# Early first projections and products across the array's halves in two recurrent stages of a fused transformer kernel

## What is computed

```python
z_na, z_gla, z_rw = hn @ w[:, :2048], hn @ w[:, 2048:3616], hn @ w[:, 3616:]
# gated linear attention, two directions, 4 heads (dk 64, dv 128), chunks of 64 tokens
b = cumsum(log_sigmoid(gd @ g_up + g_b) / 16)          # gd: the low-rank columns of z_gla
qe, ke, kd = q * exp(b), k * exp(-b), k * exp(b_last - b)
o = tril(qe @ ke.T) @ v + qe @ S_prev;  S = exp(b_last) * S_prev + kd.T @ v
# delta rule (rwkv7), two directions, 8 heads of 64
zs = conv3(z_rw)                                        # over tokens, three taps
r, k, v, wd, ad = split(zs); decay = f(tanh(wd) @ w_up); alpha = sigmoid(ad @ a_up)
S = S * w_t + (S @ a_t) b_t + v_t k_t;  y = S @ r_t
```

## Time and profile before

| | us |
|---|---|
| Three runs: median | 4121.07 |
| lowest, highest | 4120.27, 4122.79 |
| The profiled execution, its own time | 4117.64 |
| its span, first to last instruction | 4115.8 |
| PE busy in it | 3879.8 (94%) |
| DVE, ACT, POOL busy | 1526.1, 1061.7, 376.6 |
| Mean granted clock of PE | 0.977 |

### The profile page before, as it was taken

How to read it: one execution, slowest core, us unless ns; L and a number is a source line. 1 busy time by engine, 2 the same in 40 slices (tenths; PEclk the granted TensorE clock), 3 DMA queues, 4 the chain that set the end, 5 groups by cost and what they waited for, 6 DMA issues and landing times. The chain is left out here.

```text
span 4115.8 us, 64473 instructions
## 1 busy us (share of the span) xinstructions
PE 3879.8 (94%) x27772; PEld 2141.4 (52%) x27772; DVE 1526.1 (37%) x3218; ACT 1061.7 (26%) x2295; POOL 376.6 (9%) x533
## 2 busy tenths in 40 slices
PE   8999999898989889999989999999999989999998
PEld 4556755666675744544554444444444444444443
DVE  2233334464646512135658111113356547111113
ACT  2333113333343401125541000003253321000003
POOL 3340002011101000000100000000001000000000
PEclk9999999999999999999999999999999999999999
DMA  4101101000000031211048899997211148899997
GB/s 106 32 21 39 32 27 42 13 18 13 22 9 22 4 124 57 50 37 25 1 154 314 290 329 316 314 323 257 95 44 31 51 164 316 297 326 309 324 319 247
DMA packets 320587, 567.28 MB, mean 138 GB/s; under 512 B 53504, under 2 KB 127392, under 8 KB 320304
## 3 DMA queue, kind: packets, MB, share of 16 engines
q1 hardware_dynamic: 304832, 506.01, 36.3%
q0 software_dynamic: 9504, 34.61, 3.5%
q10 hardware_dynamic: 5968, 22.55, 1.4%
HBM read 514.85 MB, written 48.23 MB: 137 GB/s over the span
## 5 line engine op out<-in xcount | busy, mean ns | idle before, releaser
L3536 PE MATMUL bank<-ring,m_picked_T 128*128 128x512 f32 x2048 | 897.2, 596 | 4.1 <-ACT m_picked_T L3619 4.1
L3536 PEld LDWEIGHTS bank<-ring,m_picked_T 128*128 128x128 f32 x2048 | 389.0, 191 | 481.4 <-issue 475.8
L3536 PE MATMUL bank<-ring,m_hidden_T 128*128 128x512 f32 x1024 | 455.3, 593 | 0.0
L3536 PEld LDWEIGHTS bank<-ring,m_hidden_T 128*128 128x128 f32 x1024 | 189.6, 190 | 215.5 <-issue 215.5
L3785 DVE TENSOR_TENSOR m_hidden<-m_hidden,bank 128x512 f32<-128x512 f32 x64 | 44.0, 687 | 506.7 <-ACT m_hidden L3625 506.7
L1561 PE MATMUL bank<-hnT,first_block 128*128 128x336 f32 (+3 forms) x544 | 180.5, 483 | 8.0 <-PEq L101 7.3
L3625 ACT ACTIVATE m_hidden<-bank 128x512 f32<-128x512 f32 x64 | 38.2, 597 | 538.9 <-PE bank L3536 538.9
L241 PE MATMUL bank<-xT,first_block 128*128 128x512 f32 x352 | 152.4, 593 | 2.6 <-ACT l_i L3264 1.7
L3915 POOL DMA_INDIRECT y_rows<-m_ys,m_tokens x30 | 47.7, 1589 | 1111.9 <-DVE m_ys L3800 1046.4
L2820 PE MATMUL bank<-xT,a_weights 128*128 128x512 f32 x320 | 142.3, 595 | 0.8 <-ACT xT L2676 0.8
L1561 PEld LDWEIGHTS bank<-hnT,first_block 128*128 128x128 f32 x544 | 102.1, 193 | 67.6 <-issue 20.9
(11 more groups left out here) (503 smaller groups left out, 6010.0 us busy)
## 6 DMA issues: line engine op xcount, KB each, us to landing
ring<-in_moe_w_gate_up SPq DMA_DIRECT2D x512, 512.0 KB, 7.5
ring<-in_moe_w_down SPq DMA_DIRECT2D x256, 512.0 KB, 4.6
first_block<-in_w_in SPq DMA_DIRECT2D x23, 512.0 KB, 3.8
w_block<-in_w_in SPq DMA_DIRECT2D x19, 512.0 KB, 3.8
x_rows<-X ACTq DMA_DIRECT2D x2, 4096.0 KB, 17.0
ring<-y_rows SPq DMA_DIRECT2D x16, 512.0 KB, 8.3
out_w<-in_w_out ACTq DMA_DIRECT2D x11, 512.0 KB, 12.5
first_block<-in_lru_w_in SPq DMA_DIRECT2D x11, 512.0 KB, 3.9
```

The source lines that it names most:

```text
L3536: m = pe.matmul(banks[j][:, :], lhsT[:, (i % 8) * P:(i % 8 + 1) * P], ring[:, i, j, :], start=i % 8 == 0, stop=i % 8 == KD - 1)
```

## The change

Three things are done.

First, the three low-rank products of GLA are issued in attention's last three turns, into banks 4, 5 and 0; GLA begins with the value products, and ACT copies the finished low-rank spans. SP's waits change with the counts.

Second, five of the six spans of the delta rule's first two blocks are issued in GLA's tail: one before the first sums, one between the sums, three behind them. The sixth is the delta rule's first product. ACT copies all six in the new stage, from banks 7, 3, 4, 5, 6, 2. Key products into banks 0 and 1 wait no longer for a raw copy; into bank 2 for all six.

Third, products across the halves stand beside diagonal ones. In GLA the transposes of the keys are written in the other half, and ACT copies them back for direction 0 by two half copies, for direction 1 straight; the values get a second copy with swapped halves (`swapped`), by two more half copies each; direction 0's outer products are diagonal, direction 1's go across with the swapped values. Scores and transposes alternate, and so do the outer products. In the chain of the delta rule the output products go across and alternate with the state's, and the chained y addition becomes two operations of 64 partitions per direction.

```diff
+LOW_BANKS = (4, 5, 0)
+RAW_BANKS = ((7, 3, 4), (5, 6, 2))
...
+        def low_rank_tensor(pe, t):
+
+            j = t - steps
+            (col, w), to = SPANS[j], LOW_BANKS[j]
+            if j == 0:
+                pe.wait_ge(*k.first_in[0].now())
+            pe.wait_ge(o_taken.sem, (2 * (steps - 2), 2 * (steps - 2), 2 * (steps - 1))[j])
+            for d in range(KD):
+                x = pe.matmul(ps[to][0:48, 0:w], low_rank(k)[:, d, :], hnT[:, d, col:col + w], start=d == 0, stop=d == KD - 1)
+            x.then_inc(*k.early.up())
...
                     scores_tensor(pe, t)
+                else:
+                    low_rank_tensor(pe, t)
...
+        def raw_tensor(pe, i, j):
+
+            col, n = SPANS[j]
+            for d in range(KD):
+                x = pe.matmul(ps[RAW_BANKS[i][j]][:, 0:n], k.first[i][:, d, :], hnT[:, d, col:col + n], start=d == 0,
+                              stop=d == KD - 1)
+            x.then_inc(*k.early.up())
...
+            if j:
                 pe.wait_ge(turn_copied.sem, 5 * p + j)
...
             for i, ch in enumerate(chunks_of(j)):
                 for d in range(2):
-                    for h in HALF:
-                        x = pe.matmul(t[h, d, i, :], ke[d][h, tokens(ch)], c["ident"][h, h])
-            x.then_inc(*turned.up())
+                    for h in range(2):
+                        if j:
+                            x = pe.matmul(b[HALF[h], d, i, :], ke[d][HALF[h], tokens(ch)], qe[d][HALF[h], tokens(ch)])
+                        y = pe.matmul(t[HALF[1 - h], d, i, :], ke[d][HALF[h], tokens(ch)], c["ident"][HALF[h], HALF[h]])
...
-            for d in range(2):
-                for i, ch in enumerate(chunks_of(j)):
-                    for h in HALF:
-                        x = pe.matmul(ps[5 + d][h, i * P:i * P + P], kT[(5 * p + j) % 2][h, d, i, :], V[p][h, ch, :])
-                x.then_inc(*outer.up())
+            for i, ch in enumerate(chunks_of(j)):
+                for h in range(2):
+                    x = pe.matmul(ps[5][HALF[h], i * P:i * P + P], kT[(5 * p + j) % 2][HALF[h], 0, i, :], V[p][HALF[h], ch, :])
+                    y = pe.matmul(ps[6][HALF[h], i * P:i * P + P], kT[(5 * p + j) % 2][HALF[1 - h], 1, i, :],
+                                  swapped[p][HALF[1 - h], ch, :])
...
         def tensor(pe):
-            gd_tensor(pe)
             v_tensor(pe, 0, 0)
...
-            sum_tensor(pe, 1)
+            pe.wait_ge(*k.first_in[0].now())
+            raw_tensor(pe, 0, 0)
+            sum_tensor(pe, 1, [0])
+            pe.wait_ge(o_copied.sem, 6)
+            pe.wait_ge(squared.sem, 6)
+            raw_tensor(pe, 0, 1)
+            sum_tensor(pe, 1, [1])
+            raw_tensor(pe, 0, 2)
+            pe.wait_ge(o_copied.sem, 8)
+            pe.wait_ge(squared.sem, 8)
+            pe.wait_ge(*k.first_in[1].now())
+            raw_tensor(pe, 1, 0)
+            raw_tensor(pe, 1, 1)
...
+            ac.activation(V[p][:, chunks, :], b, ACT.Copy)
+            ac.activation(swapped[p][HALF[0], chunks, :], b[HALF[1]], ACT.Copy)
+            ac.activation(swapped[p][HALF[1], chunks, :], b[HALF[0]], ACT.Copy).then_inc(*done("v", p, j, 0))
...
+            for h in range(2):
+                ac.activation(kT[(5 * p + j) % 2][HALF[h], 0, 0:n, :], t[HALF[1 - h], 0], ACT.Copy)
+            ac.activation(kT[(5 * p + j) % 2][:, 1, 0:n, :], t[:, 1], ACT.Copy).then_inc(*turn_copied.up())
...
             cols = [RW0 + 3 * BW, RW0 + 3 * BW + P]
-            ends = [3, 6]
+            ends = [0, 1]
...
-                pe.wait_ge(copied.sem, 1 + j)
+                pe.wait_ge(copied.sem, 6 if j == 2 else 1)
...
                     pe.matmul(s_bank[HALF[h], d, :], L.P1[HALF[h], d, at[d], :], S[HALF[h], d, :])
-            for d in range(2):
-                for h in range(2):
-                    x = pe.matmul(y_bank[HALF[h], d, at[d], :], S[HALF[h], d, :], L.Q[HALF[h], d, at[d], :])
+                    x = pe.matmul(y_bank[HALF[1 - h], d, at[d], :], S[HALF[h], d, :], L.Q[HALF[h], d, at[d], :])
...
-            for i in range(2):
-                block_tensor(pe, i, ps[3 * i:3 * i + 3], enumerate(SPANS))
+            block_tensor(pe, 1, [ps[x] for x in RAW_BANKS[1]], [(2, SPANS[2])])
...
+                if chained:
+                    ve.tensor_tensor(part[HALF[0]], bank[HALF[1]], part[HALF[0]], ALU.add)
+                    ve.tensor_tensor(part[HALF[1]], bank[HALF[0]], part[HALF[1]], ALU.add).then_inc(*y_added.up())
```

More of the change, by code:

```diff
@@ L783, in gla_branch @@
         wb = [k.first[1]] + [st.sb(f"w_block{i}", [P, KD, P]) for i in range(1, 3)]
-        wv, w_low, ahead = st.sb("w_values", [P, KD, 2 * P]), low_rank(k), k.first_in[0].now()
+        wv = st.sb("w_values", [P, KD, 2 * P])
         gd, up = st.sb("gla_gd", [48, COLS]), st.sb("gla_up", [48, 2 * P])
@@ L817, in bank @@
         def bank(*name):
-            return ps[number[name] % 3]
+            return ps[(number[name] + 1) % 3]
         def reads(name):
@@ L865, in load_block, with next_block @@
             sp.dma_start(wb[i % 3][:, :, :], w3[:, :, blocks[i][2]:blocks[i][2] + P]).then_inc(*w_in[i % 3].up(16))
-        def next_block(sp, i, unit):
-            sp.wait_ge(made.sem, unit + 1)
+        def next_block(sp, i):
+            if i:
+                sp.wait_ge(made.sem, last_unit(max(b for b in range(len(blocks)) if b % 3 == 0)) + 1)
             col = RW0 + 3 * BW + i * P
@@ L893, in sync @@
             load_values(sp, 1)
-            next_block(sp, 0, number["gd", 0, 2, 0])
+            next_block(sp, 0)
             for i in range(3, len(blocks)):
                 load_block(sp, i)
-            next_block(sp, 1, last_unit(max(i for i in range(len(blocks)) if i % 3 == 0)))
+            next_block(sp, 1)
             for p in range(PAIRS):
@@ L1019, in read_tensor, with sum_tensor @@
             x.then_inc(*read.up())
-        def sum_tensor(pe, p):
-            for j in range(2):
+        def sum_tensor(pe, p, spans=range(2)):
+            for j in spans:
                 for h in range(2):
@@ L1081, in v_scalar @@
             n = len(chunks_of(j))
[L1082 to L1083 removed]
+            chunks, b = slice(chunks_of(j)[0], chunks_of(j)[-1] + 1), bank("v", p, j, 0)[:, 0:n * P].rearrange("p (c v) -> p c v", v=P)
+            ac.activation(V[p][:, chunks, :], b, ACT.Copy)
+            ac.activation(swapped[p][HALF[0], chunks, :], b[HALF[1]], ACT.Copy)
+            ac.activation(swapped[p][HALF[1], chunks, :], b[HALF[0]], ACT.Copy).then_inc(*done("v", p, j, 0))
         def log_scalar(ac, p, d):
@@ L1136, in scalar @@
             for j, (col, n) in enumerate(SPANS):
-                ready(ac, "gd", 0, j, 0)
-                ac.activation(gd[:, col:col + n], bank("gd", 0, j, 0)[0:48, 0:n], ACT.Copy).then_inc(*done("gd", 0, j, 0))
+                ac.wait_ge(k.early.sem, j + 1)
+                ac.activation(gd[:, col:col + n], ps[LOW_BANKS[j]][0:48, 0:n], ACT.Copy).then_inc(*gd_copied.up())
             for j in range(2):
@@ L1437, in spans_done @@
         def spans_done(p, block):
-            return 6 + 11 * p + (3, 6, 9, 11)[block]
+            return 1 + 11 * p + (3, 6, 9, 11)[block]
         def copies_done(p, block):
@@ L2188, in scalar @@
             ac.wait_ge(padded.sem, 8)
-            for j in range(2):
-                copy_raw(ac, temps(0)[1 + j], ps[3 * j:3 * j + 3], 3 * j, copied)
+            for i in range(2):
+                for j, (col, n) in enumerate(SPANS):
+                    if (i, j) == (1, 2):
+                        ac.wait_ge(projected.sem, 1)
+                    else:
+                        ac.wait_ge(k.early.sem, 3 + 3 * i + j + 1)
+                    ac.activation(temps(0)[1 + i][:, 1 + col:1 + col + n], ps[RAW_BANKS[i][j]][:, 0:n], ACT.Copy).then_inc(*copied.up())
             ac.wait_ge(mixed_in.sem, 3)
```

47 lines of the change are left out of this document (17 added, 30 removed).

## The result

The changed kernel takes 4099.4 us (median of four, 4098.6 to 4101.8) against 4121.9 (4120.3 to 4123.4): ratio 0.9948, 95% interval 0.9932 to 0.9964, that is 22.5 us less, with 15 to 28 inside the interval. I had put 34 less, 4087, with a range of 4075 to 4102. The sign and the range hold, a third of the gain is missing. At the first product behind the delta rule (1470.01 before, 1451.99 after) the two traces are 18.0 apart; the rest of the program, which the change does not touch, ran 2.3 us longer in the changed trace.

What follows compares the result with a forecast made beforehand. TensorE (PE), busy 94% of the span, was taken as the bound. Terms -2.7 -8.7 -14.8 -7.8 = -34.0 took the profiled 4117.64 us to 4083.6; with 3.4 for the median, 4087, range 4075 to 4102.

Steps and rivals of the forecast that it cites:

- Products across the halves: GLA's score, transpose and outer products: four quarters in a round double the pace, -14.8 us.
- Rival 1: GLA and chain: neighbours sharing a row group wait for each other, so nothing doubles; 4113 us, chance 0.09.
- rival 4: Quarter products in the new order run one at a time, making the kernel slower: 4170 us, chance 0.03.
- Second border: GLA to delta rule: five spans issued early remove PE's pause of 7.3 us; -8.7 us in all.
- rival 3: Second border: the stage's preamble or key weights come late, five of the 8.7 us lost; 4092 us, chance 0.03.
- First border: Attention to GLA: three low-rank products move ahead of the border, V products then end earlier; -2.7 us in all.
- +0.5: First border: two added half copies of V delay the second low product about 1.2 us; net cost 0.5 us.
- rival 2: GLA: ACT's added copies make it the bound, up to 15 us lost; 4102 us, chance 0.07.
- The chain: Delta rule's chain: 64 steps go from 8 rounds to 4, 14.9 us saved, not all arriving; -7.8 us.
- 3.7 x 3/4 + 3.5: Chain: 3.7 us saved by main-loop steps followed by PE's own work, 3.5 between pairs after y additions.
- (c): Chain's last eight steps: savings partly doubled by half clock, less the costs of y additions; 0.6 us gained.
- 0.7 for the last y and 0.3 for an earlier y: Chain's end: cost in us of divided y additions, the earlier one standing ahead of the inverse's addition.

Runs made afterwards that it cites:

- gla_only: Kernel before, with products across the halves and their copies in the gated linear attention alone: 4106.2 us, ratio 0.9965.
- the two repairs: Changed kernel, with either the key block's first two spans not waiting for the first raw copy (4090.8 us) or POOL's padding written before its masks (4090.2 us).
- burst: Kernel before, plus 2688 extra quarter products in eight orders and widths behind GLA's last sums, results unused: four quarters at 64 columns 16 ns busy a record.
- y_split: Kernel before, chain left on the diagonal, each chained y addition divided into two on half the partitions: 4123.3 us, ratio 1.0010.
- chain_only: Kernel before, with only the delta rule's chain changed, four quarters in a round and divided y additions: 4116.3 us, ratio 0.9986.
- chain_back: Changed kernel, with the delta rule's chain on the diagonal again in all pairs and y additions undivided: 4102.8 us, ratio 0.9953.
- both: Changed kernel, key block's first two spans waiting for no raw copy and V bank free after the first copy: 4089.3 us, ratio 0.9927.
- all_diag: Kernel `both`, with all four pairs' chains on the diagonal and no divided y addition: 4098.6 us, ratio 0.9939.
- k_free: Changed kernel, the key block's first two spans no longer waiting for ACT's first raw copy: 4090.8 us, ratio 0.9925.
- the dense run above: Last run inside `burst`, 1024 products on four quarters at 64 columns: 56.10 us for 2053 records, 27 ns a record.

## Why the prediction was right and where it was wrong

**Products across the halves: right.** Forecast -14.8. From the first group of score products to the last sums the trace shows 626.71 - 456.93 before and 611.18 - 456.16 after (where the first early projection now stands), 14.76 less, and the same in every kernel that has these products; each round holds four, a group of scores and transposes saves 0.93 and an outer group 0.87, and `gla_only` measured 14.4. Rival 1 and rival 4 fall with it, and so does the row-group rule of the Trainium skill, "TensorE: Matmul & The Clock Gate", Part 3 (The mechanism), for this order: sharing rows or not gave the same 16 ns.

**Second border: the pause went, the gain did not.** Forecast -8.7, measured -1.3 (from the last sums' start to the low-rank products 55.47 before, 54.17 after), and -8.3 with either of the two repairs. The step that failed is "ACT's first raw copy waits for POOL's padding until 8.6 us after the stage's start ... then end at 671.2, two microseconds before they are wanted". It asked when the convolutions are wanted and not who else waits for the copies: the diff had `copied.sem, 6 if j == 2 else 1` for the key block, in plain sight. That is rival 3, which I gave 0.03 and five of 8.7 us; it took 7.4. Barrier, last span, weights and key block were right to 0.1: with the wait gone it is 19.06 us, forecast 19.0.

**First border: short by 3.5.** Forecast -2.7; from record 1900, in the attention's tail, to the second low product of pair 1 the changed kernel takes 0.8 us more than before. The pause was right; the stage begins 1.4 late against my sum. The term "+0.5" for the V copies was mis-sized: alone they cost 1.0 (`gla_only` 99.9 against 98.9; but `burst`, without them, has 99.4), and beside the early products 2 to 3. With the bank freed early the border gives -1.7 to -2.6, close to my sum. This is the small, local form of rival 2. Its large form falls: no other wait on those copies shows.

**The chain: two parts right, the last wrong.** In the first three pairs I had 3.7 x 3/4 + 3.5 = 6.3 and measured 6.9. For the last pair, loop and (c), I had -1.5 and measured +2.3. The terms "0.7 for the last y and 0.3 for an earlier y" are 1.14 and 1.27 (2.4 against 1.2, 2.2 against 0.9): the last pair has no other pair's projections behind which DVE's additions could hide. And there is more time at half clock in that pair, 18 us on average against 11; the divided additions alone do not bring it (`y_split` has 10), and what sets it off was not tried. In sum -4.6 by the means, forecast -7.8. The whole times say much the same of the whole chain: 5.8 (`chain_only`), 2 (the changed kernel against `chain_back`) and 5 (`both` against `all_diag`) by the ratios, the first with some 4 us of doubt, the others with 8.

The parts as measured, +0.8 -1.3 -14.8 -4.6, make -19.9, within the interval of the measured -22.5. Two mis-sized terms and one overlooked wait make up the difference to -34. The two traces themselves also hold 1.6 us between the first border and the first scores (before, 3.4 us at half clock; after, none), which is scatter, as `k_free` shows. That the range held is in part luck: its high end was made for a chain that saves nothing or for ACT's 15 us, and what used it up was above all a wait that I had given 0.03. The measured 4099.4 lies 2.6 below that end.

## What to carry to other kernels

When work is moved ahead of a stage's border, follow each of the next stage's waits back to its releaser: whatever used to be ready before it was wanted (here POOL's padding, queued behind its masks) may now be late, and a wait that once cost nothing may guard nothing. Order a stage's setup by who wants it first. A trick that divides another engine's work, as the additions to y, belongs only where that engine has cover: here, by the means, it pays in three pairs and costs in the fourth.

## What the runs showed that was not expected

PE's instructions reach it in blocks: that is how three things read together, a stall at every 128th product record, no releaser for it, and the queue below. In the dense run above, 128 product records and their weight loads take 3.45 to 3.75 us to arrive, 27 ns a record, just under the pace of two quarters (29) and well over that of four (15 to 16). The queue for instructions on the page, before and with the burst (packets, MB, share):
```profile
q8 instruction: 220, 3.60, 0.4%
```
```profile
q8 instruction: 262, 4.29, 0.4%
```
42 packets more for 10752 records more, 256 records in a packet of 16 KB, that is 128 products and their 128 weight loads. The kernel before met this too: in the delta rule PE stands still for some 40 us with no releaser, at the same records in both kernels (records 6245, 6372, 7134 and 8024 before, 6242, 6370, 7132 and 8021 after, a few missing from each trace). Four quarters pay in GLA, where long products stand between the groups (128 V records of 56 ns or 16 gate records of 440): from the first scores to the last sums PE has no stall over 0.15 us, before or after the change. In a long unbroken run of 64-column products they would win, by the figures above, 2 ns of 29.
